# Weight sums on VectorE, last additions in the PSUM banks, state columns on ScalarE, in the gate and up stage of a hybrid encoder step

## What is computed

```python
h = rmsnorm(x, norm_ffn_g)
gt, ffn_buf_new = causal_dwconv(h @ w_gate, ffn_buf, ffn_conv_w)   # width 3
x = x + (jax.nn.silu(gt) * (h @ w_up)) @ w_down
```

## Time and profile before

| | us |
|---|---|
| Median of 3 executions | 985.41 (983.95 to 986.25) |
| The profiled execution | 985.31 |
| Its span | 983.6 |
| TensorE matmul busy in the span | 960.5 (98%) |
| VectorE busy | 667.2 (68%) |
| ScalarE busy | 433.4 (44%) |
| GpSimd busy | 227.1 (23%) |

### The profile page before, as it was taken

The page is one execution under the profiler, slowest core; times in us unless marked ns, Lnnn a source line. Parts: engine busy times, 40 slices in busy tenths (PEclk is TensorE's granted clock), DMA queues, the critical chain, the costliest instruction groups (busy, mean ns, idle before and its releaser), DMA issues.

```text
span 983.6 us, 16640 instructions
## 1 busy us (share of the span) xinstructions
PE 960.5 (98%) x6831; PEld 862.2 (88%) x6831; DVE 667.2 (68%) x1087; ACT 433.4 (44%) x751; POOL 227.1 (23%) x223
## 2 busy tenths in 40 slices
PE   9999999999999999999999999999999999999998
PEld 8898888999898877889889999999999999888887
DVE  7627886776665455661666999999999984435431
ACT  6633444648543345453654444343444443324320
POOL 0331000103553232000002055554445500000000
PEclk9999999999999999999999999999999999999999
DMA  8724242121104066044813322222122252113131
GB/s 295 245 62 129 85 131 85 44 93 45 43 4 130 1 196 217 17 161 146 319 58 113 126 85 87 86 87 84 58 74 87 86 193 95 59 49 128 45 117 53
DMA packets 73818, 103.68 MB, mean 105 GB/s; under 512 B 2576, under 2 KB 53904, under 8 KB 73360
## 3 DMA queue, kind: packets, MB, share of 16 engines
q1 hardware_dynamic: 73744, 102.63, 31.3%
HBM read 92.27 MB, written 10.35 MB: 104 GB/s over the span
## 4 chain that ended last, share of the span: by engine, by line
PE 67%; DVE 20%; issue 10%; ACT 2%; DMA 1%; POOL 0%; SPq 0%; DVEq 0%; ACTq 0%
PE bank L457 7%; PE bank L516 6%; PE bank L517 6%; PE bank L518 6%; PE bank L489 5%; PE bank L491 4%; PE bank L490 4%; PE bank L810 2%; DVE u L2642 2%; DVE act L2639 2%; DVE act L2194 2%; DVE act L2196 2%; PE bank L544 2%; PE bank L542 2%; PE bank L543 2%
## 5 line engine op out<-in xcount | busy, mean ns | idle before, releaser
L2097 DVE TENSOR_TENSOR wlo<-wraw,whi 128x2048 fp32r<-128x2048 f32 (+1 forms) x56 | 126.0, 2250 | 95.9 <-ACT whi L1561 95.9
L1561 ACT ACTIVATE whi<-wraw 128x2048 fp32r<-128x2048 f32 (+1 forms) x58 | 109.4, 1886 | 112.5 <-PE bank L518 73.5
L489 PE MATMUL bank<-hhi,whi 128*128 128x320 f32 x352 | 114.3, 325 | 0.0
L491 PE MATMUL bank<-hhi,wlo 128*128 128x320 f32 x352 | 109.5, 311 | 0.0
L490 PE MATMUL bank<-hlo,whi 128*128 128x320 f32 x352 | 109.3, 311 | 0.0
L489 PEld LDWEIGHTS bank<-hhi,whi 128*128 128x128 f32 x352 | 66.8, 190 | 9.9 <-issue 9.4
L490 PEld LDWEIGHTS bank<-hlo,whi 128*128 128x128 f32 x352 | 66.7, 190 | 1.2 <-issue 1.2
L491 PEld LDWEIGHTS bank<-hhi,wlo 128*128 128x128 f32 x352 | 66.6, 189 | 0.0
L516 PE MATMUL bank<-whi,hhi 128*128 128x512 f32 x160 | 62.2, 389 | 0.0
L517 PE MATMUL bank<-wlo,hhi 128*128 128x512 f32 x160 | 62.2, 389 | 0.0
L518 PE MATMUL bank<-whi,hlo 128*128 128x512 f32 x160 | 62.2, 389 | 0.0
(11 more groups left out here) (471 smaller groups left out, 2674.2 us busy)
## 6 DMA issues: line engine op xcount, KB each, us to landing
wraw<-in_w_in SPq DMA_DIRECT2D x13, 1024.0 KB, 5.2
wraw<-in_w_gate SPq DMA_DIRECT2D x11, 1024.0 KB, 5.1
wraw<-in_w_up SPq DMA_DIRECT2D x11, 1024.0 KB, 5.1
wraw<-in_w_down SPq DMA_DIRECT2D x10, 1024.0 KB, 5.0
kTs<-in_cache_sb_k SPq DMA_DIRECT2D x8, 512.0 KB, 4.5
vraw<-in_cache_sb_v SPq DMA_DIRECT2D x8, 512.0 KB, 5.1
wraw<-in_w_mix_out SPq DMA_DIRECT2D x4, 1024.0 KB, 6.6
kmT<-in_cache_mem_k SPq DMA_DIRECT2D x8, 512.0 KB, 6.0
```

The lines of the kernel that those rows point to most:

```text
L489: T.matmul(o, wh[:, k, cs], hhi[:, k, hs], start=(k == 0), stop=False)
L491: ins = T.matmul(o, wl[:, k, cs], hhi[:, k, hs], start=False, stop=(k == KD - 1))
L1561: V(wv(whi, i), wv(wraw, i), ACT.Copy).then_inc(s["w_hi_ready"], 1)
L2097: V.tensor_tensor(wv(wlo, i), wv(wraw, i), wv(whi, i).bitcast(F32), ALU.subtract)\
```

## The change

1. The sums of the gates' weights (j = 2 to 9) go from GpSimd to VectorE: a `weight_sums` of the same four instructions, called for j + 1 in `gate_rest` after the last addition into `cb` and ahead of the two `gate_conv` (and, for j + 1 = 2, after the convolutions of j = 1). GpSimd keeps the sums of the up blocks.
2. In `up_rest` the last addition is written into the bank it reads, and `times` reads that bank. The tile u4 is gone. A bank is given free behind the multiplication, no longer behind the addition.
3. For j = 2 to 9 ScalarE copies the state columns into `fcst` ahead of its first tap, and the cached rows into `cb` ahead of `whi` of the up block. VectorE no longer does. For the other j nothing moves.

```diff
 # GpSimd
             weight_sums("up", 1)
-            pool.wait_ge(s["rows_kept"], 16)
             for j in SEVEN["gate"]:
-                weight_sums("gate", j)
                 weight_sums("up", j)
 # ScalarE, first_tap
                 first = PAD - 2
+                V(fcst[:, ct, 0:2], t[:, PAD + SEQ - 2:PAD + SEQ], ACT.Copy)
+                V(fcst[:, ct, 2:].rearrange("p (b t) -> p b t", b=DEC_BATCH), conv_s(t)[:, :, PAD + DEC_SEQ - 2:], ACT.Copy)
                 V(out[:, 0:SEQ], t[:, first:first + SEQ], ACT.Copy, scale=w)
...
                 if j in SEVEN["gate"]:
                     first_copy("gate", j, v1)
+                    e.wait_ge(s["ffn_conv"], 2 * j)
+                    for c in range(2):
+                        V(conv_s(cb[c])[:, :, PAD - 2:PAD], cacheF[:, 2 * j + c, :].rearrange("p (b t) -> p b t", b=DEC_BATCH), ACT.Copy)
 # VectorE
+            def weight_sums(kind, j):
+
+                i, t = gu_block(kind, j), traw[kind]
+                dve.wait_ge(w_loaded[i % 3], 16 * (i // 3 + 1))
+                passed(dve, gu_block(kind, j - 1))
+                if kind == "gate" and seventh(kind, j) == 1:
+                    dve.wait_ge(s["rows_kept"], 16)
+                w = wv(wraw, i)
+                V.tensor_tensor(t[:, 0], corner(w, 0, 1), corner(w, 0, 0), ALU.subtract)
+                V.tensor_tensor(corner(w, 0, 1), corner(w, 1, 1), corner(w, 0, 1), ALU.subtract).then_inc(s["traw_" + kind], 1)
+                dve.wait_ge(s["traw_" + kind], 2 * seventh(kind, j) - 1)
+                link(V.tensor_tensor(t[:, 1], corner(w, 1, 1), t[:, 0], ALU.subtract))
+                V.tensor_tensor(t[:, 2], corner(w, 1, 0), t[:, 1], ALU.subtract).then_inc(s["traw_" + kind], 1)
...
                 b = filled(dve, (name, "p5"))
-                plus(u4[:, :], u3[:, :], b)
-                plus(u2[:, :], u2[:, :], b).then_inc(bank_free[b], 1)
-                evacuated(dve, (name, "p5"))
+                plus(u2[:, :], u2[:, :], b)
+                link(plus(bank[b][:, 0:HALF], u3[:, :], b))
                 dve.wait_ge(s["ffn_silu"], 2 * j + 2)
-                times(2 * j + 1, 1, u4[:, :])
+                times(2 * j + 1, 1, bank[b][:, 0:HALF]).then_inc(bank_free[b], 1)
                 for c, h, t in ((0, 0, u1), (0, 1, u3), (1, 0, u2)):
                     b = filled(dve, (name, c, h))
-                    link(plus(t[:, :], t[:, :], b))
-                    times(2 * j + c, h, t[:, :]).then_inc(bank_free[b], 1)
+                    link(plus(bank[b][:, 0:HALF], t[:, :], b))
+                    times(2 * j + c, h, bank[b][:, 0:HALF]).then_inc(bank_free[b], 1)
...
-                for c in range(2):
-                    pads(cb[c], cacheF[:, 2 * j + c, :], 2)
...
+                if j + 1 in SEVEN["gate"]:
+                    weight_sums("gate", j + 1)
                 for c in range(2):
                     gate_conv(2 * j + c)
```

More of the change, by code:

```diff
@@ L175, in hybrid_step @@
         u1, u2, u3 = [at(f"u{n + 1}", [P, HALF], R5 + 3328 + 15360 + HALF * 4 * n) for n in range(3)]
-        u4 = at("u4", [P, HALF], RF + 3 * TILE)
         v1, v2, v3 = [at(f"v{n + 1}", [P, HALF], R0 + 12288 + HALF * 4 * n) for n in range(3)]
@@ L2182, in conv @@
                 keep_n = taps - 1
-                V.tensor_copy(state[:, 0:keep_n], t[:, PAD + SEQ - keep_n:PAD + SEQ])
-                V.tensor_copy(state[:, keep_n:].rearrange("p (b t) -> p b t", b=DEC_BATCH),
-                              ts[:, :, PAD + DEC_SEQ - keep_n:])
                 if taken:
                     dve.wait_ge(s["tap_ready"], taken)
+                else:
+                    V.tensor_copy(state[:, 0:keep_n], t[:, PAD + SEQ - keep_n:PAD + SEQ])
+                    V.tensor_copy(state[:, keep_n:].rearrange("p (b t) -> p b t", b=DEC_BATCH),
+                                  ts[:, :, PAD + DEC_SEQ - keep_n:])
                 for k in range(1 if taken else 0, taps):
```

## The result

The changed kernel takes 971.55 us in the median of four executions (970.83 to 972.59). The kernel before, beside it, takes 983.95 to 986.25 in three executions; a fourth, of 1572.42 us, stands apart and is in neither the median of 985.41 nor the ratio. The ratio is 0.9862, with an interval of 0.9843 to 0.9882: 1.4% faster. The profiled execution took 970.83 against 985.31 before, 14.48 us less, its span 969.1 against 983.6. The forecast was 970.7.

A forecast was written before the change was run, and what follows sets the result against it. VectorE, full in turns of 26.44 us, would fall to 22.7 (20.66 - 0.70 + 2.65 + 0.10), under TensorE's 24.64; 14.6 us off 985.31 gives 970.7, forecast 969.3 to 972.5 (0.74), wider range 969.2 to 975.0.

The forecast's parts named there:

- The bound: Eight turns, j = 2 to 9: 26.44 us each against TensorE's 24.64, so 14.4 to 14.8 us can be won.
- VectorE's load: VectorE's queue time in a turn: 22.7 us undisturbed, 23.4 with `tlo_gate` held as now, under TensorE's 24.64.
- sums: Four 128x512 gate sums on VectorE: 0.61 us each, 2.65 a turn with two waits; bounds 2.4 and 5.5.
- the bank addition: Last additions of `up_rest`, written into their banks: 0.48 us each, as for an operation that reads a bank.
- the wait on itself: VectorE waiting on its own earlier instruction: one wait more for additions in their banks, 0.1 us a turn.
- the rival that needed 0.76 more for each: Dear bank writes: above 0.76 us more per addition the kernel is slower, 993 at 1.0 more; slower 0.04.
- The sign for it: In the turns VectorE would be busy for about 19 of 20 us, idling once or twice a turn for TensorE.
- The timeline of a turn: From the gate's first product: `wlo` wanted at 24.6, made by 22.5; `tlo_gate` wanted at 26.4, made by 24.7 or 25.4.
- what `wlo` of the up block waits for: End of a turn: two GpSimd sums, then `whi` at about 29.2; VectorE no more than 0.5 us late.
- The rival of moved collisions: Up block's `wlo` against GpSimd's third and fourth sum: 971 or 981.8 us; collisions or late sums, 972.5 to 983: 0.14.
- The first turn: The only close turn: `tlo_gate` of j = 2 would end some 0.4 us ahead of its need.
- The copies: Copies moved to ScalarE: 0.70 us a turn off VectorE; six small ScalarE instructions at 0.219, 1.3 us a turn.

The follow-up runs named there:

- e5: Changed kernel plus four idle 128x512 GpSimd subtractions that read SBUF, where the gates' sums had been: 990.16 us, ratio 1.0041 to the kernel before.
- e2: Kernel before with only the up block's last additions ending in their banks; gates' sums on GpSimd, copies on VectorE: 977.76 us, ratio 0.9919.
- e3: Kernel before with only the copies of state columns and cached rows moved to ScalarE: 981.78 us, ratio 0.9951.
- e4: Changed kernel with the copies back on VectorE, so sums and banks only: 970.81 us, ratio 0.9848 to the kernel before.
- e6: Changed kernel plus ten 128x512 GpSimd memsets, which read nothing, where the gates' sums had been: 973.63 us, ratio 0.9877 to the kernel before.
- e7: Changed kernel with the up block's additions ending in SBUF tiles again, so sums and copies only: 972.78 us, ratio 0.9873 to the kernel before.
- e1: Kernel before with only the gates' sums moved to VectorE; additions end in SBUF tiles, copies on VectorE: 975.85 us, ratio 0.9903.

## Why the prediction was right, and where its steps were off

**The bound.** The argument that 14.4 to 14.8 us could be won, and no more, held: 14.5 in the span, 14.6 in the stage. It rests on the length of a turn against TensorE's own pace, and that pace was met exactly, 24.64.

**VectorE's load.** The prediction had 22.7 us, or 23.4 with `tlo_gate` held. Measured in the turn above: 24.64 - 1.02 - 0.90 = 22.72, with `tlo_gate` not held. Single terms: sums 2.65, measured 2.66; the bank addition 0.48, measured 0.49; the wait on itself 0.1, measured 0.52 - 0.41 = 0.11, the start-to-start distance of addition to multiplication less that of multiplication to addition. The estimate that a write into a bank costs what a read does was right, and the rival that needed 0.76 more for each falls.

**The sign for it was mis-stated.** "VectorE is busy for about 19 of 20 us" doesn't follow from a load of 22.7: that is 22.72 / 24.64 x 20 = 18.4. The window shows 17.80, less again for two reasons: both idle times of a turn fall into these 20 us, 1.01 + 0.91, and the short gaps between instructions, some 0.3 us, count as load and not as busy.

**The timeline of a turn.** `tlo_gate` was expected at 24.7 or, held, 25.4 after the gate's first product. It is clean, since VectorE, done earlier, starts it before GpSimd's up sums: 638.42, against 640.35 here.

```profile
640.35 1.30 POOL L1526 TENSOR_TENSOR traw_up<-wraw 128x512 f32<-128x512 f32 x1 [19.33 <-PE bank L1174]
...
644.37 1.31 POOL L1530 TENSOR_TENSOR traw_up<-wraw,traw_up 128x512 f32<-128x512 f32 x1
```

This order is what decides: in e5 it is turned round and costs 0.57.

**The step that failed: what `wlo` of the up block waits for.** The prediction had it wait for two sums and `whi`, "no more than 0.5 late". It waits for all four sums (`cut_lo`, line 2097 of the changed kernel), which I had not read there. `whi` is ready before that:

```profile
643.03 1.92 ACT L1558 ACTIVATE whi<-wraw 128x2048 fp32r<-128x2048 f32 x1 [0.38 <-POOL wraw L1527]
```

It ends at 644.95, the fourth sum at 645.68, and `wlo` starts at 645.71. The wait is 1.02 us and its cause another. It cost nothing, because VectorE had 1.92 us in a turn to spare. The prediction had not set aside room for it, so that part is luck: an estimate with a load of 24 us in place of 22.7 gives a turn of 25.0 if the wait stayed as long, some 3 us more in eight turns.

**The rival of moved collisions** (971 to 981.8) named this very place, `wlo` of the up block against GpSimd's third and fourth sum. They can't collide, by the same wait: `wlo` starts when the fourth sum has ended. That VectorE's instructions can collide with GpSimd's elsewhere is what e2 and e5 show.

**The first turn.** `tlo_gate` of j = 2 was to be 0.4 us ahead of its need; it is 0.3 late, the one wait that is left. Some of it is that `wlo` of this block waits 0.29 us for `whi` (at 587.88), which the prediction had not counted.

**The copies.** ScalarE takes the state copies in 0.11 us of queue time each, 651.45 to 651.67 for two, against the 0.219 that I took:

```profile
651.45 0.20 ACT L2023 ACTIVATE fcst<-cb 128x2 f32<-128x2 f32 x1 [4.25 <-DVE cb L2690]
651.56 0.20 ACT L2024 ACTIVATE fcst<-cb 128x16 f32<-128x16 f32 x1
651.67 0.71 ACT L2025 ACTIVATE act<-cb,flanes 128x512 f32<-128x512 f32 x1
```

e3 shows that they are worth 0.69 a turn where VectorE is the bound, and e4 that they are worth nothing where it isn't.

**The mechanism.** That it is GpSimd's reads that hold VectorE's instructions with all inputs in SBUF is shown by e5 and e6 together, at nearly the same length of GpSimd's work (5.66 and 5.81 us). The Trainium skill ("SBUF — State Buffer", Who interferes with whom) says so of two SBUF inputs and a GpSimd operation that reads, and that issue order decides who blocks; e2's two turns, 0.50 us and 0.03 us apart, agree. The same section of the Trainium skill names `copy` and `tensor_scalar` as operations that can also contend through a 2-port mode; the 0.17 that became 0.46 under memsets agrees, while the operations with two tensor inputs stayed at their time.

The Trainium skill ("Perfetto Trace Analysis", Optimizing Scalar/DVE Operations) has a higher overhead of VectorE on PSUM than on SBUF, by which, as an estimate, the four multiplications would have cost 0.26 us more. The trace doesn't show it: 0.49 us with a bank, and 0.49 for an undisturbed multiplication by a u tile in the kernel before (at 651.93).

## What to carry to other kernels

Measure the length of a turn from start to start, and the pace of the engine that should be the bound where nothing holds it: their difference times the turns is all that a change can give there, and parts that each give much alone will together give no more. TensorE's granted clock can fall inside the stage, as it did during the wait of e5's first turn, so look at it before a difference is put down to waits alone. Where VectorE and GpSimd work at the same time, look at every VectorE instruction that has its tensor inputs in SBUF alone and see whether it takes its clean time; it can be freed by a bank as an input, by GpSimd writing without reading, or by starting first (0.50 us ahead was enough in e2; GpSimd was enough ahead with 0.03). Of the three parts here any two give 12.9 to 14.6 of the 14.6 us in the stage.

## What the runs showed of the hardware that I had not expected

- Starts 0.03 us apart, as the profile times them, decide which of the two engines waits, and the second waits for nearly all that is left of the first's instruction: 1.12 us of 1.27 for VectorE in the one case, 1.11 of 1.26 for GpSimd in the other (e2).
- Beside memsets on GpSimd, which read nothing, the profile shows longer instructions of two kinds: a VectorE copy of 128x2 goes from 0.17 to 0.46 us and a `tensor_scalar` of 128x128 from 0.28 to 0.62 (e6). The `tensor_tensor` of 128x512 stays at 0.69 and the `scalar_tensor_tensor` at 0.75.
- VectorE writing a bank that it also reads takes 0.49 us for 128x320, as much as with an SBUF tile as its output.
- With VectorE busy for 19.69 of 20 us TensorE still isn't held (e7); with 19.65 it is, in every turn (e1).
- During a wait of TensorE's of 3.9 us the granted clock fell to 0.50 and stayed there for some 7 us, with matmuls 0.267 us apart in place of 0.147 (e5). In one of ten executions of that kernel the mean clock was 1.000, so there it can't have fallen for long.
